# Strassen's identity in the FFN products of a decoder layer on eight cores

## What is computed

```python
def swiglu(h, w_gate, w_up, w_down):
    return (jax.nn.silu(h @ w_gate) * (h @ w_up)) @ w_down
...
x = x + 0.5 * swiglu(rms_norm(x, ffn1_norm), ffn1_w_gate, ffn1_w_up, ffn1_w_down)
h = rms_norm(x, mix_norm)
z = h @ w_in                       # 2304 columns: q, k, v, conv u, gates
attn = sliding_window_sink_attention(q, k, v, sinks, rel_table)
conv = gate_b * causal_short_conv(gate_c * u, conv_w)
x = x + concat(rms_norm(attn), rms_norm(conv)) @ w_out
x = x + 0.5 * swiglu(rms_norm(x, ffn2_norm), ffn2_w_gate, ffn2_w_up, ffn2_w_down)
return rms_norm(x, final_norm)
```

## Time and profile before

| | |
|---|---|
| device time, three runs | 1294.35, 1294.79, 1296.77 us (median 1294.79) |
| profiled execution, span of the slowest core (6) | 1295.2 us |
| spans of the eight cores | 1281.1 to 1295.2 us |
| busy: TensorE, DVE, ACT, Pool | 95%, 36%, 25%, 13% |
| chain that ended last: TensorE, DMA, DVE, ACT | 85%, 8%, 3%, 2% |

### The profile page before, as it was taken

The page is one execution under the profiler, slowest core; times in us unless marked ns, Lnnn a source line. Parts: engine busy times, 40 slices in busy tenths (PEclk is TensorE's granted clock), DMA queues, the critical chain, the costliest instruction groups (busy, mean ns, idle before and its releaser), DMA issues.

```text
span 1295.2 us, 18401 instructions; the slowest of 8 cores (1281.1 to 1295.2 us)
## 1 busy us (share of the span) xinstructions
PE 1229.3 (95%) x6474; PEld 612.4 (47%) x6564; DVE 462.7 (36%) x791; ACT 320.8 (25%) x539; POOL 169.5 (13%) x324
## 2 busy tenths in 40 slices
PE   3899999999998999999999799999999999999996
PEld 1566656656554444444444344444444444444442
DVE  2623232253345523141273222313424552314125
ACT  3310101143444310101441001013344431010122
POOL 2011102102000121102111011110200012110200
PEclk9999999999998999999999989999999999999998
DMA  8653527417321873728429755362623146272713
GB/s 238 114 90 54 86 33 106 66 17 106 50 34 25 195 100 45 109 33 122 66 36 191 213 88 78 51 103 40 99 42 48 25 67 99 42 112 33 122 25 130
DMA packets 59352, 107.98 MB, mean 83 GB/s; under 512 B 5888, under 2 KB 11136, under 8 KB 59136
## 3 DMA queue, kind: packets, MB, share of 16 engines
q0 software_dynamic: 45504, 82.86, 42.5%
q1 hardware_dynamic: 12080, 20.71, 5.2%
q10 hardware_dynamic: 1680, 3.24, 0.8%
HBM read 181.24 MB, written 8.39 MB: 146 GB/s over the span
## 4 chain that ended last, share of the span: by engine, by line
PE 85%; DMA 8%; DVE 3%; ACT 2%; issue 2%; POOL 0%; SPq 0%; DVEq 0%; ACTq 0%; POOLq 0%
PE psall L485 43%; PE psall L546 23%; PE psall L574 8%; DMA outT<-xT_sb 4%; PE psall L840 4%; DMA ring_sb<-ws 2%; DMA xT_sb<-xT 2%; PE psall L349 2%; PE psall L490 1%; PE psall L734 1%; PE psall L733 1%; PE psall L663 1%; DVE xT_sb L415 1%; PE psall L610 1%; PE psall L729 1%
## 5 line engine op out<-in xcount | busy, mean ns | idle before, releaser
L485 PE MATMUL psall<-hT_sb,ring_sb 128*128 128x512 bf16 (+1 forms) x3055 | 616.1, 362 | 6.9 <-DMA ring_sb<-ws 4.0
L485 PEld LDWEIGHTS psall<-hT_sb,ring_sb 128*128 128x128 bf16 x3096 | 302.8, 98 | 317.2 <-issue 8.1
L546 PE MATMUL psall<-aT_sb,ring_sb 128*128 128x512 bf16 (+1 forms) x1561 | 320.3, 365 | 9.9 <-DVE xT_sb L553 8.6
L253 POOL DMA_DIRECT2D ring_sb<-ws x316 | 167.0, 538 | 1069.7 <-PE psall L485 413.0
L502 DVE TENSOR_TENSOR aT_sb<-psall,sS_sb 128x512 bf16<-128x512 f32 (+1 forms) x198 | 128.1, 647 | 463.4 <-PE psall L485 448.5
L500 ACT ACTIVATE sS_sb<-psall 128x512 f32<-128x512 f32 (+1 forms) x198 | 111.1, 561 | 704.9 <-PE psall L485 663.9
L546 PEld LDWEIGHTS psall<-aT_sb,ring_sb 128*128 128x128 bf16 x1584 | 155.6, 98 | 171.8 <-issue 16.3
L553 DVE SCALAR_TENSOR_TENSOR xT_sb<-psall,xT_sb 128x512 f32<-128x512 f32 (+1 forms) x216 | 139.7, 647 | 175.4 <-PE psall L546 162.0
L574 PE MATMUL psall<-hT_sb,ring_sb 128*128 128x384 bf16 (+3 forms) x675 | 126.4, 341 | 1.8 <-DVE rden_sb L759 0.8
L574 PEld LDWEIGHTS psall<-hT_sb,ring_sb 128*128 128x128 bf16 x680 | 66.4, 99 | 56.0 <-issue 6.1
L363 DVE SCALAR_TENSOR_TENSOR hT_sb<-xT_sb,gains_sb,psall 128x384 bf16<-128x384 f32 (+1 forms) x96 | 59.7, 675 | 33.0 <-ACT psall L354 30.1
(11 more groups left out here) (76 smaller groups left out, 375.9 us busy)
## 6 DMA issues: line engine op xcount, KB each, us to landing
ring_sb<-ws POOLq DMA_DIRECT2D x316, 256.0 KB, 5.4
outT<-xT_sb SPq DMA_DIRECT2D x6, 1024.0 KB, 17.2
xT_sb<-xT SPq DMA_DIRECT2D x2, 2048.0 KB, 18.5
xT_sb<-xT SPq DMA_DIRECT2D x2, 1536.0 KB, 31.1
convT_sb<-xT SPq DMA_DIRECT2D x1, 2048.0 KB, 12.7
outT<-xT_sb SPq DMA_DIRECT2D x4, 512.0 KB, 3.0
EB_sb<-biasT ACTq DMA_DIRECT2D x1, 1024.0 KB, 17.3
EB_sb<-xT SPq DMA_DIRECT2D x1, 1024.0 KB, 15.8
```

What stands on the lines that cost most here:

```text
L253: S.op("pool", lambda e, slot=slot, ci=ci: e.dma_start(out=ring[:, slot, :], in_=ws_d[ci]), writes=[("ring", slot)], dma=ringsem[slot], ex ...
L485: inst = e.matmul(ps[b][:, 0:n], lhsT=ring[:, s, kc * 128:(kc + 1) * 128], rhs=hT[:, kc, t0:t0 + n], start=(kc == 0), stop=(kc == 7))
L546: inst = e.matmul(ps[b][:, 0:n], lhsT=ring[:, s, o * 128:(o + 1) * 128], rhs=aT[:, fl, t0:t0 + n], start=(fl == 0), stop=(fl == len(dslots ...
```

## The change

The FFN products are made in two-by-two blocks by Strassen's identity (in Winograd's form). For the gate and up products of two inner blocks at a time (a pair), the blocks are the 1024 input features in two halves of four blocks, the two inner blocks, and the two token tiles of 512. The eight block products of such a two-by-two multiplication become seven, on sums of blocks. `GROUPS` now are 3, 3, 3 and 2 pairs.

- Weight sums: a slot of the new ring (`w0_sb` to `w6_sb`, seven slots of 128 x 7 x 512) gets four blocks by one transfer of 128 x 2048; three sums are made on Pool (`w_sums`), the fourth on DVE, in place (`w_s3`).
- Sums of h (`h_sums`, DVE, 4 operations of 128 x 2048 before an FFN) in `ht_sb`, and of the inner activations (`a_sums`, DVE, 4 of 128 x 512 a pair) in `a_sb`.
- Sums of the results: in PSUM by accumulation, where ACT copies a bank's intermediate value out (`act_copy`) before more is added to it; by a matmul of a stored copy with the identity (`inject`, L508); and by DVE from a bank and a copy (`dve_add`, `xadd_sb`).
- `part1` makes products 1 and 2 of gate and up, `part2` the other five; `down_couple` makes the down products of a group for two of the four couples of output blocks. The first FFN's first two pairs (`plain_t`) and the last group's down products (`down_plain`) stay as ordinary products.
- At an FFN's start, except the first, `part1` of all three pairs comes before the first `part2`.
- The halo of 128 tokens leaves the tiles and gets matmuls of 128 columns of its own (L620, L720).
- Each half of the tokens has a buffer for x of its own (`x0_sb`, `x1_sb`); the mixer's buffers lie in the one that is free. The second half's x is loaded in the first half's second FFN, and its sums of squares are made there (`between2`).

```diff
-GROUPS = [list(range(0, 7)), list(range(7, 14)), list(range(14, 22))]
...
+NSLOT = 7
+NPAIR = 11
+GROUPS = [[0, 1, 2], [3, 4, 5], [6, 7, 8], [9, 10]]
...
+        def w_sums(upto):
+            while st_["summed"] < min(upto, st_["issued"]):
+                n = st_["summed"]
+                st_["summed"] += 1
+                if not entry_sums(n):
+                    continue
+                w = W[n % NSLOT]
+
+                def add(eng, o, i0, i1, op, w=w):
+                    S.op(eng, lambda e: e.tensor_tensor(out=w[:, o, :], in0=w[:, i0, :], in1=w[:, i1, :], op=op),
+                         reads=[w.k(i0), w.k(i1)], writes=[w.k(o)])
+                add("pool", 4, 2, 3, ALU.add)
+                add("pool", 5, 4, 0, ALU.subtract)
+                add("pool", 6, 1, 5, ALU.subtract)
+
+        def w_s3(n):
+            w = W[n % NSLOT]
+            S.op("dve", lambda e: e.tensor_tensor(out=w[:, 2, :], in0=w[:, 0, :], in1=w[:, 2, :], op=ALU.subtract),
+                 reads=[w.k(0), w.k(2)], writes=[w.k(2)])
+
+        SUMLAG = 2
...
+        def h_sums():
+
+            def f(o, i0, i1):
+                S.op("dve", lambda e: e.tensor_tensor(out=o[0], in0=i0[0], in1=i1[0], op=ALU.subtract),
...
+                return (ht[:, i], ht.k(i))
...
+        PROD = {1: (0, ("q", 0)), 2: (1, ("q", 2)), 3: (6, ("q", 3)), 4: (3, ("t", 2)), 5: (4, ("t", 0)), 6: (5, ("t", 1)), 7: (2, ("q", 1))}
...
+        def inject(b, p1):
+            need("setup")
+            S.op("pe", lambda e: e.matmul(ps[b], lhsT=identb[:], rhs=p1[:], start=False, stop=True, skip_group_check=True),
+                 reads=[identb.k(), p1.k()], writes=[PB(b)])
+
+        def act_copy(o, b, scale=1.0):
+            S.op("act", lambda e: e.activation(out=o[:], in_=ps[b], func=AF.Copy, scale=scale), reads=[PB(b)], writes=[o.k()])
...
+            def part1(j, wg, wu, pb):
+                pg, pu = p1b[2 * pb], p1b[2 * pb + 1]
+                gprod(wg, 0, 1, True, False)
+                act_copy(pg, 0)
+                gprod(wu, 3, 1, True, False)
+                act_copy(pu, 3)
+                gprod(wg, 0, 2, False, True)
+                gprod(wu, 3, 2, False, True)
+                s = next_sl()
+                silu(s, ps[0], PB(0))
+                amul(j, 0, ps[3], PB(3), s)
+                drain(1)
+
+            def part2(j, wg, wu, pb):
+                pg, pu = p1b[2 * pb], p1b[2 * pb + 1]
+                gprod(wg, 1, 6, True, False)
+                inject(1, pg)
+                act_copy(u2b[0], 1)
+                gprod(wu, 4, 6, True, False)
+                inject(4, pu)
+                act_copy(u2b[1], 4)
+                gprod(wg, 2, 5, True, False)
+                gprod(wu, 5, 5, True, False)
+                drain(2)
+                gprod(wg, 1, 7, False, False)
+                act_copy(u3b[0], 1)
+                gprod(wu, 4, 7, False, False)
+                act_copy(u3b[1], 4)
+                dve_add(u3b[0], 2, u3b[0])
+                dve_add(u3b[1], 5, u3b[1])
+                gprod(wg, 1, 4, False, True)
+                silu(u3b[0], u3b[0][:], u3b[0].k())
+                s = next_sl()
+                gprod(wg, 2, 3, False, True)
+                silu(s, ps[1], PB(1))
+                dve_add(u2b[0], 2, u2b[0])
+                silu(u2b[0], u2b[0][:], u2b[0].k())
+                amul(j, 3, u3b[1][:], u3b[1].k(), u3b[0])
+                gprod(wu, 4, 4, False, True)
+                gprod(wu, 5, 3, False, True)
+                amul(j, 2, ps[4], PB(4), s)
+                dve_add(u2b[1], 5, u2b[1])
+                amul(j, 1, u2b[1][:], u2b[1].k(), u2b[0])
...
+            def a_sums(j):
+                def f(o, i0, i1):
+                    S.op("dve", lambda e: e.tensor_tensor(out=A[:, j, o, :], in0=A[:, j, i0, :], in1=A[:, j, i1, :], op=ALU.subtract),
+                         reads=[A.k(j, i0), A.k(j, i1)], writes=[A.k(j, o)])
+                f(4, 1, 0)
+                f(5, 3, 4)
+                f(6, 2, 5)
+                f(1, 3, 1)
...
+                def prod(si, P, js, start, stop):
+                    b = 3 * si + {1: 0, 2: 0, 6: 1, 7: 1, 4: 1, 5: 2, 3: 2}[P]
+                    wi, which = PROD[P]
+                    aq = AQ[which]
+                    o = couple[si]
+
+                    def mm(e):
...
+                for si in range(2):
+                    prod(si, 1, al, True, False)
+                    act_copy(p1b[si], 3 * si)
+                for si in range(2):
+                    prod(si, 6, al[:-1], True, False)
+                    prod(si, 5, al[:-1], True, False)
+                for si in range(2):
+                    prod(si, 2, al, False, True)
+                    xadd(3 * si, couple[si], 0)
+                for si in range(2):
+                    prod(si, 6, al[-1:], False, False)
+                    inject(3 * si + 1, p1b[si])
+                    act_copy(u2b[si], 3 * si + 1, 0.5)
+                for si in range(2):
+                    prod(si, 5, al[-1:], False, False)
+                    xadd(3 * si + 2, 4 + couple[si], 1)
+                for si in range(2):
+                    prod(si, 7, al, False, False)
+                    act_copy(u3b[si], 3 * si + 1, 0.5)
+                    xadd_sb(u2b[si], couple[si], 1)
+                for si in range(2):
+                    prod(si, 4, al, False, True)
+                    prod(si, 3, al, False, True)
+                    xadd_sb(u3b[si], 4 + couple[si], 1)
+                    xadd(3 * si + 1, 4 + couple[si], 0)
+                    xadd(3 * si + 2, couple[si], 1)
+                drain(1)
...
+            def lead_mid2(x=x):
+                r = norm_stats(1, 7)
+                for kc in range(8):
+                    h_mul(x, kc, 1, G_FFN2, r)
+                for f in h_sums():
...
+                        if t is not None:
+                            for kc in range(8):
+                                q = sqb[st_["sq"] % 2]
+                                st_["sq"] += 1
+                                S.op("act", lambda e, kc=kc, q=q: e.activation(out=q[:], in_=x1[:, t, kc, :], func=AF.Square),
+                                     reads=[x1.k(t, kc)], writes=[q.k()])
+                                S.op("pe", lambda e, kc=kc, q=q: e.matmul(ps[6 + t], lhsT=ones[:], rhs=q[:], start=(kc == 0), stop=(kc == 7)),
+                                     reads=[q.k(), ones.k()], writes=[PB(6 + t)])
+                            pre[t] = next_rs()
+                            rstd_of(6 + t, 512, 1.0 / D, pre[t])
...
-        def ffn(tag, tiles, pendA, pendB, sqrow, doneB, done_last_inside, hook=None):
-            def phase1(fl, sg, su, t0, n, mid=None, fine=False):
...
-                    for kc in range(8):
-                        inst = e.matmul(ps[b][:, 0:n], lhsT=ring[:, s, kc * 128:(kc + 1) * 128],
-                                        rhs=hT[:, kc, t0:t0 + n], start=(kc == 0), stop=(kc == 7))
...
-                sb_i = state["sS"]
...
-                     reads=[("ps", bg)], writes=[("sS", sb_i)])
-                S.op("dve", lambda e: e.tensor_tensor(out=aT[:, fl, t0:t0 + n], in0=ps[bu][:, 0:n], in1=sS[:, sb_i, 0:n], op=ALU.mult),
-                     reads=[("ps", bu), ("sS", sb_i)], writes=blk_keys("a", t0, n, fl))
-                drain_dve(4)
```

1640 lines of the change are left out of this document (915 added, 725 removed).

## The result

| | median, us | runs |
|---|---|---|
| before | 1295.7 | 1294.4 to 1297.0 |
| after | 1460.6 | 1458.2 to 1474.1 |

The ratio is 1.130, with a 95% interval of 1.125 to 1.135.

A forecast was written before the change was run, and what follows sets the result against it. TensorE, 95% busy and never waiting in the FFNs, was taken as the bound; 1295.2 - 70.0 - 13.1 + 11.5 + 11.8 + 4 + 7.5 + 10 + 4 + 5 = 1266 us, range 1240 to 1345.

The forecast's parts named there:

- What is removed: TensorE's matmuls: fewer 512-wide products in the FFNs, all other matmuls growing by 1.7 us; net -70.0 us.
- Collisions of DVE with Pool: Rival, chance 0.18: after every pair, DVE operations with both inputs in SBUF wait for Pool's sums; at worst 1357 us.
- Its x: Time a DVE operation with two SBUF inputs waits for Pool: 0.44 us eats the gain, 0.67 costs 91 us.
- The layout, start and order: Second half's x -13.1 us, second FFN's squares +10, halo squares +4, bias and last normalisation +5, start 0.
- The -13.1: From 680 to 760 us: loss from waiting for the second half's x goes, given its own buffer and earlier load.
- The start: First 50 us: as much work done as before, though x's second tile is asked for late; 0, bounds -4 and +8.
- Hand-overs: TensorE waits around ACT's bank copies: 0.27 us in 42 pairs, +11.5; 0.49 in 24 down couples, +11.8.
- At an FFN's start: Three of four FFNs: ACT's and DVE's work takes 9.7 us against 7.2 of cover by 32 matmuls; +7.5 us.
- At a down start: Twelve places where DVE is still behind: no wait with fast sums, but +4 us taken for bias and normalisation work.
- DVE at 0.69 on 16-bit data: Rival, chance 0.17: DVE's SBUF sums take 0.69 us instead of 0.42, costing at down and FFN starts; 1289 us.
- the table loads for Copy: Rival, chance 0.04: Copy is not in silu's table, so ACT makes four table loads a pair; +109 us, 1375.
- Hidden hand-overs: Rival, chance 0.07: TensorE's hand-over waits are covered and the start is quicker; 1233 us.

The follow-up runs named there:

- the plain one: The changed kernel with plain products in all FFNs, no sums anywhere, in the new layout: 1343.9 us, ratio 1.036.

## Why the prediction was wrong

On core 1 the change costs 1448.7 - 1282.0 = 166.7 us, and the kernels above split it: -69 of TensorE's work, +48 of layout, start and order (109 - 61), +76 of Strassen's hand-overs and starts (185 - 109), +112 of Pool's sums (297 - 185).

**What is removed.** Right: 6564 to 6132 matmuls, -69 us for -70.0.

**Collisions of DVE with Pool: the step that failed.** I gave the rival 0.18 and the sum nothing. What I held against it, that Pool idles 0.17 us between dependent sums, is too short for a DVE operation to matter: the traces show DVE's sums of a stepping one to a Pool sum. The rival's own price was near. Its x is the extra of an operation: 0.65 us for the sums of a, 0.51 for the multiplications from SBUF, 0.21 for the weight differences. At x = 0.67 it gave 91 us; measured, 112 in the span and 121 in the time. In part that nearness is luck: its five operations took some 0.6 us more each, by which its formula gives 42 x 1.1 + 12 x 2.6 = 77 us; other operations that were held up and matmuls at the lower clock make up the rest, in shares that I haven't traced. That it is collisions is shown by three kernels: without the sums, with Pool writing only, and with the sums beside work that reads PSUM. What I had quoted from the Trainium skill ("SBUF — State Buffer", who interferes with whom) was the mechanism, and no row spoke against it.

**The layout, start and order** I had at -13.1 + 10 + 4 + 5 + 0 = +6; they are +48. The -13.1 was read on core 6, the slowest, where TensorE waited 8.6 us in two places, 5.67 of them in the earlier trace rows. On core 1 it was one wait of 2.8:

```profile
PE psall L546 <- DVE xT_sb L553: 2.8, 1, 2.8
```

The other six had 1.0 to 6.5. The start, which I had at 0 with a bound of +8, waits until 43.9 us in the changed kernel (40.7 in the plain one) for x's second tile's squares and again for the halo's; up to the first mixer's scores the plain kernel is 26.2 us behind before (345.0 for 318.8 us). Moving the weight blocks and the halo's squares gave back 9.2 of these on core 1. The halo's squares after the first FFN cost 8.8 us, not 4. Another 28 of the 54 us between the two spans arise behind the first mixer's scores. Among them are the squares of x between the pairs of the second FFN (some 3 us for each of two tiles in the plain kernel; some 6 in the one without Pool's sums, where matmuls at the lower clock follow; I had 5), a wait of 6.0 us for DVE's normalisation products where the second mixer begins, and 8.1 us of waits for the squares of the last normalisation, where the kernel before has 2.1. The remainder I haven't traced.

**Hand-overs** were mis-sized a little. In the kernel without Pool's sums the rows of TensorE give the periods:

```profile
567.63 4.70 PE L658 MATMUL psall<-a_sb,w_sb 128*128 128x512 bf16 x21
...
587.87 3.81 PE L538 MATMUL psall<-hq_sb,w_sb 128*128 128x512 bf16 x16
591.52 1.03 PE L538 MATMUL psall<-ht_sb,w_sb 128*128 128x512 bf16 x4
...
604.36 1.03 PE L538 MATMUL psall<-ht_sb,w_sb 128*128 128x512 bf16 x4
```

From 591.52 to 604.36 one pair takes 12.84 us for 12.52 of work: 0.32, where I had 0.27. From 567.63 to 587.87 two couples of 44 take 20.24 for 18.99: 0.62 each, where I had 0.49. Then the first sixteen matmuls of the next pair take 3.65 for 3.45. Over 42 pairs and 24 couples that is some 30 us for 23.3.

**At an FFN's start** I was wrong by a factor of five. From the first product, at 454.79, to the first behind the three pairs' first halves, at 480.22, the same kernel takes 25.4 us for 12.1 of work (48 products and 8 statistics matmuls): 13.3. The other two starts, read in the same way, lose 10.8 and 12.1: 36 in all, where I had 7.5 (the plain kernel's starts lose 1.6 at most). I took the three pairs' 32 matmuls behind the statistics for cover and did not see that the last 12 wait for a bank which DVE's queue holds. I had also left out ACT's table loads there: from the end of the statistics to DVE's first product are 3.0 us, where I had 1.5. 30 + 36 is most of the 76.

**At a down start** I had 4 us; without collisions no wait is recorded there. With them eight waits for the sums of a and eleven for weight differences come to 29 us.

**The rivals.** DVE at 0.69 on 16-bit data and the table loads for Copy are refuted: 0.36 to 0.43 for a sum, 1.22 for one over 2048, and 21 table loads, none at a copy. Hidden hand-overs are too.

## What to carry to other kernels

Before work is put on Pool beside a busy DVE, list which DVE operations have all their operands in SBUF and which Pool operations read: every such pair that meets costs DVE up to a whole Pool operation (here 0.4 us became 1.1 to 1.4), and everything behind it in DVE's queue waits too. It can then be quicker to give DVE the work itself.

When TensorE is 95% busy, a saving of matmuls is worth only what its new waits leave: here 75 us of products fewer brought 4, since 0.3 us in each of 42 pairs, 0.6 in each of 24 couples and 11 to 13 at each of three starts took the rest. For each stretch of cover ask which banks it needs and behind what the operation that frees them is queued.

A wait that is read on the slowest core is not what the kernel gains when it goes; look at the same wait on the other cores.

## What the hardware showed that I had not expected

Operations of DVE with one tensor operand, in SBUF, are held up too: the diagonal products took 994 ns for 284, and the one cast of 128 elements to identb 0.57 us for 0.22, both with Pool's sums beside them. Beside memsets the diagonal products took 1422 ns, the cast 0.22. I had listed only operations with two, and only Pool operations that read. The Trainium skill (same section) names casts and tensor_scalar too, where they run in a two-port mode; no row shows the mode, but for the diagonal products the trace agrees, 994 ns beside sums, 1422 beside memsets and 284 without.

Pool is hardly slowed by DVE: its sum takes 1178 ns beside plain products and 1202 to 1214 beside Strassen's.

The lower clock level followed waits as short as 2.1 us in places and not in others: behind one of 2.10 us at an FFN's start eight matmuls took 3.56 us, behind one of 2.24 in a pair 1.89. Which it will be I can't say from these rows.
